# Two-layer decoder step: first value tile evicted before the exponentials, three projection tiles behind the block selection, the first keys in other banks, the sample scaling and its store moved up

## The reference

```python
h = rms_norm(x, g_mix[l])
proj = jnp.einsum('bld,de->ble', h, w_in[l])
rq, rk, rv, rg, mq, mk, mv, gate_r, gate_a = split_proj(proj)
rq = retnet_rotate(rq, pos); rk = retnet_rotate(rk, pos) * (R_DK ** -0.5)
ro, r_state = ret_mix(l, rq, rk, rv)          # retention
mq = rope(mq, pos); mk = rope(mk, pos)
mo = attn_mix(l, mq, mk, mv)                   # block-sparse attention
merged = sigmoid(gate_r) * (ro @ w_br_ret[l]) + sigmoid(gate_a) * (mo @ w_br_att[l])
x = x + merged @ w_out[l]
x = x + (silu(gu[..., :D_FF]) * gu[..., D_FF:]) @ w_down[l]    # gu = rms_norm(x, g_ffn) @ w_gu
```

## Time and profile before

| | us |
|---|---|
| median of 3 runs (lowest, highest) | 2104.92 (2103.58, 2107.37) |
| the profiled execution | 2102.82 |
| its span, first to last instruction | 2101.2 |
| TensorE busy in the span | 2036.8 |
| VectorE, ScalarE, GpSimd busy | 971.9, 685.6, 127.8 |
| layer 0 from its first product to layer 1's | 24 to 1054 |

### The profile page before, as it was taken

The page is one execution under the profiler, slowest core; times in us unless marked ns, Lnnn a source line. Parts: engine busy times, 40 slices in busy tenths (PEclk is TensorE's granted clock), DMA queues, the critical chain, the costliest instruction groups (busy, mean ns, idle before and its releaser), DMA issues.

```text
span 2101.2 us, 45106 instructions
## 1 busy us (share of the span) xinstructions
PE 2036.8 (97%) x17393; PEld 1911.9 (91%) x17393; DVE 971.9 (46%) x1620; ACT 685.6 (33%) x1054; POOL 127.8 (6%) x211
## 2 busy tenths in 40 slices
PE   7989999999999999999999899999999999999999
PEld 6958878988999999999988688799899999999998
DVE  6473513456445544543364643133654554444433
ACT  4365423223222222222233654223232322222222
POOL 0001120011000000000000011200100000000000
PEclk9999999999999999999999999999999999999999
DMA  5316683245332232223343266812543333232222
GB/s 192 121 44 215 195 265 111 81 141 171 115 108 82 80 100 80 82 75 89 95 149 123 79 206 203 288 50 93 163 149 102 92 86 95 80 93 74 83 82 90
DMA packets 257967, 253.20 MB, mean 121 GB/s; under 512 B 12266, under 2 KB 223378, under 8 KB 257554
## 3 DMA queue, kind: packets, MB, share of 16 engines
q1 hardware_dynamic: 237970, 190.42, 29.2%
q0 software_dynamic: 17632, 60.31, 9.0%
q10 hardware_dynamic: 2208, 0.41, 0.1%
HBM read 230.52 MB, written 20.58 MB: 120 GB/s over the span
## 4 chain that ended last, share of the span: by engine, by line
PE 91%; DVE 2%; ACT 2%; issue 2%; DMA 1%; ACTq 0%; POOL 0%; DVEq 0%; SPq 0%; POOLq 0%
PE PS L633 62%; PE PS L614 3%; PE PS L615 3%; PE PS L616 3%; PE PS L779 2%; PE PS L595 2%; PE PS L596 2%; PE PS L597 2%; PE PS L838 2%; PE PS L790 1%; PE PS L574 1%; PE PS L666 1%; PE PS L728 1%; DMA PG<-in_cache_k 1%; ACT WH L1057 1%
## 5 line engine op out<-in xcount | busy, mean ns | idle before, releaser
L633 PE MATMUL PS<-XH,WH 128*128 128x272 f32 x2176 | 454.6, 290 | 5.0 <-DVE EA L1712 3.1
L633 PE MATMUL PS<-XH,WL 128*128 128x272 f32 x2176 | 450.4, 288 | 0.0
L633 PE MATMUL PS<-XL,WH 128*128 128x272 f32 x2176 | 448.8, 288 | 0.0
L1421 DVE TENSOR_TENSOR WL<-RAW,WH 128x2048 fp32r<-128x2048 f32 (+2 forms) x144 | 310.7, 2158 | 235.2 <-ACT WH L1057 234.5
L633 PEld LDWEIGHTS PS<-XH,WH 128*128 128x128 f32 x2176 | 342.1, 188 | 12.6 <-DVE EA L1712 8.2
L633 PEld LDWEIGHTS PS<-XL,WH 128*128 128x128 f32 x2176 | 341.9, 188 | 0.0
L633 PEld LDWEIGHTS PS<-XH,WL 128*128 128x128 f32 x2176 | 339.8, 189 | 0.0
L1057 ACT ACTIVATE WH<-RAW 128x2048 fp32r<-128x2048 f32 (+2 forms) x152 | 274.6, 1807 | 98.2 <-PE PS L633 87.9
L1661 DVE TENSOR_TENSOR EA<-PS,RSTDB 128x544 f32<-128x544 f32 x120 | 86.3, 721 | 227.2 <-PE PS L633 226.5
L1258 ACT ACTIVATE EB<-EA 128x544 f32<-128x544 f32 x92 | 60.5, 658 | 329.7 <-DVE EA L1661 276.0
L614 PE MATMUL PS<-WH,XH 128*128 128x256 f32 x512 | 152.2, 297 | 5.1 <-ACT XT L1211 5.1
(11 more groups left out here) (266 smaller groups left out, 3061.8 us busy)
## 6 DMA issues: line engine op xcount, KB each, us to landing
RAW<-in_w_in SPq DMA_DIRECT2D x106, 512.0 KB, 4.5
RAW<-in_w_gu SPq DMA_DIRECT2D x88, 512.0 KB, 4.6
PG<-in_cache_k SPq DMA_DIRECT2D x64, 256.0 KB, 3.1
PG<-in_cache_k POOLq DMA_DIRECT2D x64, 256.0 KB, 3.2
RAW<-in_w_down SPq DMA_DIRECT2D x32, 384.0 KB, 3.1
PG<-in_cache_v SPq DMA_DIRECT2D x44, 256.0 KB, 3.6
PG<-in_cache_v POOLq DMA_DIRECT2D x44, 256.0 KB, 3.9
RAW<-in_w_down SPq DMA_DIRECT2D x32, 320.0 KB, 3.6
```

The lines of the kernel that those rows point to most:

```text
L633: last = pe.matmul(PS[:, 2 * pair + h, 0:HALF], w[:, i, c0:c0 + P], x[:, k, h * HALF:(h + 1) * HALF], start=first and i == 0 and a == 0, s ...
L1421: dve.tensor_tensor(WL[:, slot, 0:n], RAW[:, slot, 0:n], WH[:, slot, 0:n].bitcast(F32), ALU.subtract).then_inc(lo_ready, 1)
```

## The change

The diff has five edits; the last two follow from the others.

1. Sample scaling: the store of the sample columns goes from ScalarE's queue to SyncE's, behind the constants; VectorE waits for it and multiplies before the low part of unit mqk 1.
2. First keys: chunk c goes to bank (c+2) mod 3, so chunk 0 goes to bank 2, and TensorE waits for `mo_lo` per chunk (chunk 1 for three of four, chunk 2 for all). The high and low part of unit rqk 1 are made behind rqk tile 2 and no longer ahead of tile 1.
3. Selection: three rqk tiles (10, 11, 12) stand ahead of step 8, `filler(q)` is q+5 from there on, and step 15 has none.
4. Values: ScalarE evicts rv 0 ahead of `exp_group(1)`.
5. The load of unit rv 1 is issued one step of SyncE's page loop earlier, as tile numbers run one ahead.

```diff
-        return q + 2 if q < N_PAGES else q + 4
+        return q + 2 if q < N_PAGES else q + 5
...
             sp.dma_start(CL[:], consts_layer).then_inc(cl_in, 16)
+            hold(sp, x_lo, lay * NX + KT)
+            sp.dma_start(XTD.ap()[:, :, SEQ:N], XN).then_inc(xs_kept, 16)
...
-                                           (15, "rv", 1, C_RV), (20, "rv", 2, C_RV), (23, "rv", 3, C_RV),
+                                           (14, "rv", 1, C_RV), (20, "rv", 2, C_RV), (23, "rv", 3, C_RV),
...
                     if c >= 3:
                         pe.wait_ge(kt_act, lay * 64 + c - 2)
+                    elif c:
+                        pe.wait_ge(mo_lo, lay * 4 + 2 + c)
                     for hp in range(4):
-                        last = pe.transpose(PS[:, c % 3, hp * P:(hp + 1) * P],
+                        last = pe.transpose(PS[:, (c + 2) % 3, hp * P:(hp + 1) * P],
...
-            pe.wait_ge(mo_lo, lay * 4 + 4)
             turn_keys(0, (0, 1))
             turn_keys(0, (2, 3))
             for q in range(NG * N_PAGES):
                 if q == N_PAGES:
-                    token_part("rqk", N_PAGES + 2, kk)
-                    token_part("rqk", N_PAGES + 3, kk)
+                    for f in range(N_PAGES + 2, N_PAGES + 5):
+                        token_part("rqk", f, kk)
                 if q + 1 < NG * N_PAGES:
                     turn_keys(q + 1, (0, 1))
-                token_part("rqk", filler(q), kk[:4])
                 if q + 1 < NG * N_PAGES:
+                    token_part("rqk", filler(q), kk[:4])
                     turn_keys(q + 1, (2, 3))
-                token_part("rqk", filler(q), kk[4:])
+                    token_part("rqk", filler(q), kk[4:])
                 key_scores(q)
...
-            act.wait_ge(x_lo, lay * NX + KT)
-            act.dma_start(XTD.ap()[:, :, SEQ:N], XN).then_inc(xs_kept, 16)
...
-            sample_probs_turned(0)
-            exp_group(1)
...
+            sample_probs_turned(0)
+            value(0)
+            exp_group(1)
...
+            dve.wait_ge(xs_kept, lay * 16 + 16)
+            dve.tensor_tensor(XN, XN, GT[:, bass.ds(lay * KT, KT)].unsqueeze(2).to_broadcast([P, KT, NS]),
+                              ALU.mult).then_inc(xn_ready, 1)
             for u in range(4):
                 ahead("mqk", u // 2, u % 2)
                 if u == 0:
-                    dve.wait_ge(xs_kept, lay * 16 + 16)
-                    dve.tensor_tensor(XN, XN, GT[:, bass.ds(lay * KT, KT)].unsqueeze(2).to_broadcast([P, KT, NS]),
-                                      ALU.mult).then_inc(xn_ready, 1)
                     dve.wait_ge(cl_in, lay * 16 + 16)
```

More of the change, by code:

```diff
@@ L403, in _ @@
                 if j == 0:
-                    hold(sp, x_lo, lay * NX + KT)
                     sp.dma_start(XTD.ap()[:, :, 0:SEQ], XT[:, :, 0:SEQ]).then_inc(xt_kept, 16)
@@ L1167, in keys_turned @@
                         act.wait_ge(sc_done, lay * 18 + q - 1 + (q >= 10))
-                    act.activation(KTT[q % 2][:, b, :, :], PS[:, (4 * q + b) % 3, :].rearrange("p (k c) -> p k c", c=P),
+                    act.activation(KTT[q % 2][:, b, :, :], PS[:, (4 * q + b + 2) % 3, :].rearrange("p (k c) -> p k c", c=P),
                                    ACT.Copy).then_inc(kt_act, 1)
@@ L1184, in attended_sample @@
                                ACT.Copy).then_inc(mos_hi, 1)
-            split_at("rqk", 1)
             to_rotate(1)
@@ L1190, in _ @@
                 if q == N_PAGES:
-                    to_rotate(N_PAGES + 2)
-                    to_rotate(N_PAGES + 3)
-                if q + 1 < NG * N_PAGES:
-                    keys_turned(q + 1, range(GRP))
+                    for f in range(N_PAGES + 2, N_PAGES + 5):
+                        to_rotate(f)
+                if q + 1 == NG * N_PAGES:
+                    break
+                keys_turned(q + 1, range(GRP))
                 if q == N_PAGES:
@@ L1198, in _ @@
                 to_rotate(f)
+                if q == 0:
+                    split_at("rqk", 1)
                 if f == TT - 1:
@@ L1223, in _ @@
                     for f in value_tiles(g, p):
-                        value(f)
+                        if f:
+                            value(f)
                         if f % TT == 0:
@@ L1602, in _ @@
                     select(0)
-                    rotated(N_PAGES + 2)
-                    rotated(N_PAGES + 3)
+                    for f in range(N_PAGES + 2, N_PAGES + 5):
+                        rotated(f)
                     inverse_sum(0)
+                if q + 1 == NG * N_PAGES:
+                    break
                 f = filler(q)
                 rotated(f)
+                if q == 0:
+                    split_at("rqk", 1)
                 if f == TT - 1:
```

## The result

| | before | after |
|---|---|---|
| median (lowest to highest), us | 2104.43 (2103.58 to 2107.37) | 2092.28 (2089.63 to 2095.55) |
| span of the profiled execution | 2101.2 | 2090.6 |
| ratio of the times | | 0.9941, interval 0.9927 to 0.9956 |

The change gains 12.2 us. The direction and the places were right; one term above all was too small.

What follows compares the result with a forecast made beforehand. TensorE was taken as the bound, busy 2036.8 of 2101.2 us, only its waits removable. Terms 2.5 + 1.35 - 0.6 per layer, twice, plus 2.0 once: 8.5 off 2104.9, stated as 2096.5; forecast case 2094.5 to 2098.0 (0.62), overall range 2093.0 to 2101.0.

Steps and rivals of the forecast that it cites:

- Values, 2.5 per layer: At rv tile 2: evicting rv 0 ahead of the exponentials gains 2.5 us per layer, bounds 2.1 and 2.7.
- C: Theory formed after four runs, not predicted: a TensorE pause costs more than its length, half clock following in some executions.
- First keys, 1.35 per layer: At the first key transposes: other banks and the later split gain 1.35 us per layer, bounds 1.0 and 1.8.
- Selection, -0.6 per layer: At step 8's scores: the third tile loses 0.6 us per layer, exponentials still waiting behind four chunks; bounds -1.5 and +0.1.
- The rival in which the wait goes altogether: At step 8's scores: 1.5 us gained instead of 0.6 lost, 12.7 in all, 2092.2; chance 0.06.
- Sample scaling, 2.0 once: At layer 1's sample tile: scaling ahead of the low part gains 2.0 us, once; bounds 0 and 2.05.
- The late store: Rival at layer 1's sample tile: store lands after 1065, nothing gained there, 6.5 us in all, 2098.4; chance 0.10.
- Page waits left as they are: At TensorE's three waits on pages, 1.8 us in all, longest 0.8: assumed unchanged.
- the slower rival by pages: In 28 steps with pages: waiting 0.55 us for one pair each loses 15.4 us, giving 2111.8; chance 0.03.
- From one trace to the median: Whole kernel: profiled execution is 2.1 us below the median 2104.9, and the forecast gain was subtracted from that median.

Runs made afterwards that it cites:

- keys_only: Kernel before with only the first key chunks in other banks, a wait per chunk and unit rqk 1's split behind tile 2: 2101.57 us, ratio 0.9983.
- no_third: Changed kernel with the third rqk tile ahead of step 8 undone, so a tile stands at step 15 again: 2092.96 us, ratio 0.9944 to before.
- scaling_only: Kernel before with only the sample store moved behind the constants and the scaling ahead of the low part: 2102.8 us, ratio 0.9991.

## Why the prediction was wrong, step by step

- **Values, 2.5 per layer: the term that was mis-sized.** It measured 2.8 per layer in the trace and 7.2 in all by the ratio when made alone, where C gives 2 x 2.8 and 1.7 for the clock, less the 1.0 that rv 3 takes back, 6.3. The step that failed is "I take 2.5 per layer; the bounds are 2.1 and 2.7": it took a wait's length for its price. A wait of TensorE that long was followed by half clock in 9 of 16 layers, 1.3 to 1.5 us each, and the one trace behind the prediction had none of them, so no row of it could show the cost. The bounds should have been 2.1 and 4.2. What is late next was worked out rightly: rv 3 gives back 0.5, and only if the selection isn't earlier.
- **First keys, 1.35 per layer.** 1.6 and 1.5 in the two layers, inside the bounds: both the shorter wait (1.51 to 0.40) and the 0.31 for the first chunk went; the estimate had kept some of the second. keys_only gives 1.8 per layer by the ratio.
- **Selection, -0.6 per layer.** The mechanism was right row for row (215.45, 217.73 and 1.58 above). The cost was 0.35 and 0.26. From the scores of step 7 to those of step 8 it is 3.44 more than before (15.08 against 11.64, 208.33 to 219.96), where the sum had 3.5; what it had too small is the tile taken away at step 15, which gave back 3.2 and not 2.9. What the sum left out is the other end of the edit: without the tile at step 15 the wait of rv 3 (0.45 per layer in no_third) doesn't come back. So the edit comes out at about nothing in these runs, not at -1.2. The rival in which the wait goes altogether gave 2092.2, next to the measured time, by the wrong way: the wait is still there, at 3.1.
- **Sample scaling, 2.0 once.** 1.78 in the trace and 1.9 in scaling_only. This wait too is a number of an execution: 2.0, 1.4, 2.3 and 2.0 in the four traces of before, and 0.6 to 1.9 in five of other kernels without the edit; that 2.0 fitted was partly luck. The late store didn't happen: 1.2 us were left. The Trainium skill's page "DMA: Bandwidth & Descriptors", section "Queues, rings and completion order", has increments land only behind earlier writes of the same engine; the landings of 1054.7 and 1055.1 agree. They don't prove it: with the 3.9 that it took on its own queue the store would have landed at 1054.6.
- **Page waits left as they are.** 1.3 against 1.8; over the four traces of before they are 1.8, 0.6, 1.0 and none. They aren't a number of the kernel, but of an execution; the slower rival by pages didn't come near.
- **From one trace to the median.** The prediction took the trace's 2.1 below the median as a shift that the change leaves alone. Some of it was low clock behind the very pause that the change removes.

With the measured terms the sum is 2 x (2.8 + 1.5 - 0.3) + 1.8 = 9.8, and 1.7 for the clock behind the pause: 11.5, near the measured 12.2. Of the 3.7 us between forecast and result, 1.3 are terms that the trace had larger and 1.7 the clock; the rest is open. The interval of the whole change (9.3 to 15.4) holds 9.8 as well as 11.5, so it is the filled pause, and not the whole change's time, that shows the clock's part.

## What to carry to other kernels

A wait of a busy TensorE may cost more than its length: where the idle time is a microsecond or two, look in several traces at the granted clock behind it, and at its mean over all executions, and put the lower clock into the upper bound of what removing the wait brings. Before a long operation is given more cover on TensorE, read the list of the engine that performs it: here a third tile (2.9 us) hid none of a wait of 1.5, and moving the exponentials ahead of two evictions in ScalarE's list, with a low part of VectorE moved behind them as well, took it away. And where an edit takes work from a later place, price that place too.

## What the hardware showed that was not expected

TensorE, 97% busy over the span, was idle for 1.8 to 2.5 us in one place. In 9 of 16 such layers the granted clock then fell to 1.2 GHz for about 3.4 us (0.80 and 0.77 over two windows of 4 us), at a price of 1.3 to 1.5. With the idle time cut to 0.8 and transposes of no use in the rest, it stayed at 2.4 GHz in 4 of 4, and the kernel was 2.5 us faster for 36 more transposes. Two executions of the same kernel with the same pause of 2.53 differed in this, and no run here tells why.
